# The first norm's weight as one row spread by two matmuls, and a reordered opening

## What is computed

```
h = rmsnorm(x, norm_mix_pre)           # x * rsqrt(mean(x^2) + 1e-6) * weight, row by row
P = h @ W_in                           # 1024 x 3584: seven groups of 512 columns
yA = block-sparse causal attention (8 heads, T5 relative bias) on three groups
yR = chunked retention (8 heads, group norm, swish gate) on four groups
x = x + rmsnorm(concat(yA, yR) @ W_out, norm_mix_post)
h = rmsnorm(x, norm_ffn_pre);  u = causal conv3(h @ W_up) + conv_b
x = x + rmsnorm((gelu(u_a) * u_b) @ W_down, norm_ffn_post)
```

## Time and profile before

| | us |
|---|---|
| median of 3 runs | 658.28 |
| lowest and highest | 658.04, 659.0 |
| the profiled execution, its device time | 657.82 |
| its span in the trace | 656.0 |
| PE busy | 637.3 (97% of the span) |
| DVE, ACT, POOL busy | 384.0, 299.4, 69.1 |

### The profile page before, as it was taken

How to read it: one execution, slowest core, us unless ns; L and a number is a source line. 1 busy time by engine, 2 the same in 40 slices (tenths; PEclk the granted TensorE clock), 3 DMA queues, 4 the chain that set the end, 5 groups by cost and what they waited for, 6 DMA issues and landing times.

```text
span 656.0 us, 9379 instructions
## 1 busy us (share of the span) xinstructions
PE 637.3 (97%) x3210; PEld 526.6 (80%) x3210; DVE 384.0 (59%) x565; ACT 299.4 (46%) x485; POOL 69.1 (11%) x88
## 2 busy tenths in 40 slices
PE   7999999999999899999999999999999999999996
PEld 7887877777787687899888888888888888878885
DVE  3448548646854975985755555555555654463455
ACT  5548327526733854664433333333333433362351
POOL 5402102111210302420000000000000000000002
PEclk9999999999999999999999999999999999999999
DMA  9634223331412145641433333333333023422323
GB/s 282 189 119 128 66 64 97 96 96 32 145 47 89 72 160 161 193 129 65 129 96 96 96 96 96 96 96 96 96 95 100 29 95 97 160 64 61 96 68 128
DMA packets 87110, 69.15 MB, mean 105 GB/s; under 512 B 2265, under 2 KB 76169, under 8 KB 87090
## 3 DMA queue, kind: packets, MB, share of 16 engines
q1 hardware_dynamic: 85618, 63.62, 32.2%
q0 software_dynamic: 1472, 5.26, 2.5%
HBM read 66.76 MB, written 2.12 MB: 105 GB/s over the span
## 4 chain that ended last, share of the span: by engine, by line
PE 83%; DVE 8%; ACT 3%; issue 3%; DMA 1%; POOL 1%; DVEq 0%; SPq 0%; POOLq 0%; ACTq 0%
PE bank L435 77%; PE bank L515 1%; DVE work L1165 1%; ACT work L827 1%; DMA raw<-in_w_in_dram 1%; DVE work L1174 1%; DVE ws L1048 1%; PE bank L578 1%; DVE yT L1094 1%; DVE work L1183 1%; PE bank L506 1%; DVE work L1184 1%; PE bank L505 1%; PE bank L446 1%; POOL ws L360 1%
## 5 line engine op out<-in xcount | busy, mean ns | idle before, releaser
L435 PE MATMUL bank<-hT,ws 128*128 128x512 f32 (+1 forms) x1872 | 412.4, 376 | 5.7 <-DVE work L1183 4.3
L435 PEld LDWEIGHTS bank<-hT,ws 128*128 128x128 f32 x1872 | 327.9, 188 | 67.1 <-issue 6.7
L435 PE MATMUL bank<-ws,yT 128*128 128x512 f32 x720 | 166.7, 390 | 0.3 <-PE bank L435 0.3
L435 PEld LDWEIGHTS bank<-ws,yT 128*128 128x128 f32 x720 | 134.3, 188 | 28.4 <-issue 1.1
L1048 DVE TENSOR_TENSOR ws<-raw,ws 128x1024 fp32r<-128x1024 f32 x85 | 103.5, 1218 | 6.9 <-ACT ws L768 6.4
L768 ACT ACTIVATE ws<-raw 128x1024 fp32r<-128x1024 f32 x88 | 92.5, 1052 | 15.5 <-PE bank L435 11.7
L1327 DVE TENSOR_TENSOR ws<-raw,ws 128x1024 fp32r<-128x1024 f32 x22 | 26.9, 1224 | 51.2 <-ACT ws L1008 51.2
L985 ACT ACTIVATE gains<-bank,conv 128x512 f32<-128x512 f32 x22 | 17.1, 779 | 75.0 <-PE bank L435 75.0
L1008 ACT ACTIVATE ws<-raw 128x1024 fp32r<-128x1024 f32 x22 | 23.3, 1057 | 56.2 <-PE bank L435 56.2
L985 ACT ACTIVATE rot<-bank,conv 128x512 f32<-128x512 f32 x22 | 17.1, 779 | 67.7 <-PE bank L435 67.7
L1304 DVE SCALAR_TENSOR_TENSOR gains<-bank,conv,gains 128x511 f32<-128x511 f32 x22 | 16.5, 750 | 52.8 <-ACT gains L985 52.8
(11 more groups left out here) (111 smaller groups left out, 477.4 us busy)
## 6 DMA issues: line engine op xcount, KB each, us to landing
raw<-in_w_up_dram SPq DMA_DIRECT2D x44, 512.0 KB, 3.8
raw<-in_w_in_dram SPq DMA_DIRECT2D x28, 512.0 KB, 4.4
raw<-in_w_down_dram SPq DMA_DIRECT2D x22, 512.0 KB, 3.9
raw<-in_w_out_dram SPq DMA_DIRECT2D x16, 512.0 KB, 3.6
xs<-in_x_dram SPq DMA_DIRECT2D x4, 512.0 KB, 6.4
work<-bias_vectors POOLq DMA_DIRECT2D x4, 512.0 KB, 3.9
work<-in_decay_dram POOLq DMA_DIRECT2D x4, 512.0 KB, 4.5
out_dram<-work SPq DMA_DIRECT2D x4, 256.0 KB, 2.0
```

The lines of the kernel that those rows point to most:

```text
L435: return nc.tensor.matmul(dst, st, mv, start=start, stop=stop)
```

## The change

`norm_mix_pre` is loaded as one row of 4 KB to partition 0, by ACT's own DMA queue, ahead of ACT's first activation. PE multiplies a column of 128 ones with each half of the row (two matmuls with a contraction of one, 512 columns each) into banks 6 and 7, and DVE copies the two halves to `gains`. The 512 KB load leaves SP's queue. `POOL_TO` goes from 3 to 1, so the low parts of units 1 and 2 are made by DVE instead of POOL. The squares of x tile 3 go from ACT to DVE (`tensor_tensor_reduce`). PE's warming matmuls go from 15, 2, 8 to 3, then behind the two spreading matmuls 7, 2, 4. Unit 1's `FRONT` goes ahead of the turn of tile 2.

```diff
-POOL_TO = 3
+POOL_TO = 1
...
+        ones = work[0:1, 9728:9728 + P]
+        x_squared = part(8704, 1024)
...
@@ SP
             load_x(1)
-            sp.dma_start(gains[:, 0, :], norm_mix_pre[0].partition_broadcast(P)).then_inc(gains_loaded, 16)
             load_turn(0, 0, 1)
...
@@ POOL
+            pool.memset(ones, 1.0).then_inc(ones_set, 1)
             pool.memset(neghalf[:], -0.5).then_inc(const_set, 1)
...
             x_rstd(2)
-            split_lo(1)
             x_rstd(3)
-            split_lo(2)
...
@@ PE
-            warm(15)
+            warm(3)
+            pe.wait_ge(gains_loaded, 16)
+            pe.wait_ge(ones_set, 1)
+            for half in range(2):
+                nc.tensor.matmul(bank[6 + half][:], ones, gains[0:1, 0, half * 512:half * 512 + 512],
+                                 start=True, stop=True).then_inc(gains_spread, 1)
+            warm(7)
             turn_rows(0)
             warm(2)
             turn_rows(1)
-            warm(8)
+            warm(4)
 
             pe.wait_ge(h_lo, 4)
             pe.wait_ge(w_lo_pool, 1)
             column_unit(0, bank[0], 0, 24, FRONT, False)
+            pe.wait_ge(w_lo, lo_count(1))
+            column_unit(1, bank[1], 0, 24, FRONT, False)
             turn_rows(2)
-            pe.wait_ge(w_lo_pool, 2)
-            column_unit(1, bank[1], 0, 24, FRONT, False)
             turn_rows(3)
...
@@ ACT
+            act.dma_start(gains[0:1, 0, :], norm_mix_pre[0:1, :]).then_inc(gains_loaded, 16)
             x_in(0)
...
             split_hi(1)
-            x_in(3)
             h_evacuate(2)
...
@@ DVE
-            dve.wait_ge(gains_loaded, 16)
+            for half in range(2):
+                dve.wait_ge(gains_spread, half + 1)
+                nc.vector.tensor_copy(gains[:, 0, half * 512:half * 512 + 512], bank[6 + half][:]).then_inc(gains_ready, 1)
+            dve.wait_ge(gains_ready, 2)
             normed_rows(0)
             normed_rows(1)
             h_low(0)
             h_low(1)
+            dve.wait_ge(x_loaded[3], 16)
+            dve.wait_ge(sq_done, 3)
+            nc.vector.tensor_tensor_reduce(out=x_squared, in0=xs[:, 3, :], in1=xs[:, 3, :], scale=1.0, scalar=0.0,
+                                           op0=ALU.mult, op1=ALU.add, accum_out=sumsq[:, 3:4]).then_inc(sq_done, 1)
             normed_rows(2)
+            split_lo(1)
             normed_rows(3)
             h_low(2)
             h_low(3)
+            split_lo(2)
```

More of the change, by code:

```diff
@@ L203, in build @@
         const_set = sem("const_set")
+        ones_set, gains_spread, gains_ready = sem("ones_set"), sem("gains_spread"), sem("gains_ready")
         low_cleared = sem("low_cleared")
```

## The result

| | before | changed |
|---|---|---|
| median of 12 runs, us | 657.95 | 660.36 |
| lowest to highest | 657.38 to 659.37 | 659.38 to 660.74 |
| ratio changed : before | | 1.0028 (95%: 1.002 to 1.0037) |
| profiled execution: device time, span | 657.82, 656.0 | 659.38, 657.6 |

The kernel became slower by about 0.3%, 1.8 us by the ratio; the two medians are 2.4 us apart. The forecast was no change (658.3), with 660.36 just inside the range of 657.1 to 660.5.

A forecast was written before the change was run, and what follows sets the result against it. PE was taken to bound the kernel, with only the opening before BACK (24.10 us) open to change. The terms summed to 24.1, so no change: 658.3 us on the median, chance 0.47, range 657.1 to 660.5.

The forecast's parts named there:

- What bounds: Whole kernel: PE is busy 97% of the span, and the end moves one for one with the BACK start, 24.10.
- The load leaves the queue: Opening DMAs: 512 KB less saves 1.5 to 2.3 us, so unit 0 lands at 7.6 to 8.4 instead of 9.92.
- The row arrives: Opening, ACT's queue: the 4 KB row, issued at about 0.75, lands at 2.75 to 4.05; 3.2 taken.
- land with x: Rival, opening: the row lands only at 4.05, DVE's rows start at 7.9, and the kernel takes 658.8 us; chance 0.10.
- The two matmuls: Opening, PE: the spreading matmuls start at 3.25, PE's pace rises at about 5.6, the second ends at 6.3, or 7.0 if slow.
- Tiles 0 and 1: Opening: ACT's fourth evacuation ends (E) 4.43 us after DVE's first rows start (G, 7.4), at 11.83.
- the pace stays low: Rival, opening: PE stays slow, warming matmuls last until 10.4; 662.3 us, or 660.3 if it rises at turn 0; chance 0.09.
- POOL beside DVE: Opening, tile 2: DVE's squares delay POOL's root, so DVE's rows start 1.9 us after ACT's squares end (S), not 1.3.
- POOL is not held up: Rival, opening: DVE's squares leave POOL alone, tile 2's rows start 0.6 us earlier, 657.7 us; chance 0.20.
- Low part of unit 1, and the turn behind it: Opening: unit 1's FRONT starts at S (ACT's tile 2 squares end) + 4.45, 17.3; BACK follows 6.75 us later, before 5.59.
- POOL in between: Rival, opening: POOL's low part of unit 0 runs between DVE's first two rows, up to 2.4 us late, 660.7 us; chance 0.08.
- The sum: BACK start: DVE's rows start (G) 7.4 + 4.43 + 1.04 + 4.45 + 6.75 = 24.1, as before.

The follow-up runs named there:

- e2: The changed kernel with four warming matmuls instead of seven behind the spreading ones; median 660.38 us, ratio to before 1.0030.
- e9: The changed kernel with POOL waiting for DVE's first two rows, tile 2's turn between the units and tile 3's squares on ACT; 658.35 us, ratio to before 1.0001.
- e1: The changed kernel without the seven warming matmuls behind the spreading ones; median 660.50 us, ratio to before 1.0035.
- e4: The changed kernel with the turn of tile 2 back between the FRONTs of units 0 and 1; median 658.94 us, ratio to before 1.0010.
- e5: The kernel before with only the row on ACT's queue, the spreading matmuls and their warming matmuls; median 658.97 us, ratio to before 1.0013.
- e7: The changed kernel with POOL waiting for both of DVE's first rows before unit 0's low part; median 659.74 us, ratio to before 1.0026.
- e6: The changed kernel with the weight loaded to all partitions by SP and 15, 2 and 8 warming matmuls, as before; 659.00 us, ratio to before 1.0008.
- e3: The changed kernel with spreading matmuls over all 128 rows, the weight's tile cleared first and the row loaded later; 662.29 us, ratio to before 1.0057.
- e10: The kernel before with its first 15 warming matmuls using one row of the array instead of 128; 659.58 us, ratio to before 1.0019.
- e8: The kernel before with only the low parts of units 1 and 2 moved to DVE; median 657.50 us, ratio to before 0.9990.
- e12: The kernel before with 20 first warming matmuls instead of 15; median 657.74 us, ratio to before 0.9991.
- e11: The kernel before with units 1 and 2's low parts on DVE and 20 first warming matmuls instead of 15; 657.16 us, ratio to before 0.9983.

## Why the prediction was right or wrong

Its map of the opening held; its forecast of no change did not. The measured slowdown lies among its cases with 0.14. The range held, but by 0.14 us and with some luck: the profiled execution, 659.38, lies above the 657.8 to 659.1 that the prediction gave for it, and what the range had room for was its rivals. Two of its own signs of being wrong came up: DVE's rows started after 8 us, and the seven warming matmuls lasted over 2 us (3.34).

- **What bounds.** Right. BACK moved by 1.55 us, the span by 1.6; the waits behind are the same to 0.1 us.
- **The load leaves the queue.** Right for the profiled run, and about right in the mean: unit 0 landed at 8.25, expected 7.6 to 8.4. In six others without the load it landed at 7.54 (e2), 7.75 (e9), 7.78 (e1), 8.41 (e4), 8.52 (e5) and 9.02 (e7), a wider spread than was allowed for.
- **The row arrives.** Taken as 3.2. PE began the spreading at 3.56 without an idle gap, so it was there by then. Harmless; what moved the spreading from 3.25 to 3.56 was the three warming matmuls. That it would land with x was not borne out in this run: tile 0's squares began at 4.29, when x had landed.
- **The two matmuls: the term that failed first.** "The second is a quarter done at 5.6 and ends at 6.3" took the moment of the rise from one run with other work on PE; in five runs of the old opening it lies between 5.3 and 7.5. The second ended at 7.3, both at low pace. The prediction had the other bound, 7.9 for DVE's rows, and even that was 0.2 too early, since PE began 0.3 later: they started at 8.10. The copies cost 0.69, as read from the earlier trace rows.
- **Tiles 0 and 1: the term that failed second.** E = G + 4.43 left out the seven warming matmuls. At 0.48 each they end at 10.6, 1.2 us behind tile 0's rows. E was 13.48, G + 5.38. The rival "the pace stays low" had exactly this, but to the end of the turns, and with 0.09.
- **POOL beside DVE.** Right, and well sized. The root's second instruction took 1.43 us and ended 0.4 us behind DVE's squares; tile 2's rows started at 16.34, 1.83 us behind S = 14.51, for the 1.9 taken. "POOL is not held up" is out.
- **Low part of unit 1, and the turn behind it.** Right: S + 4.31 (4.45 taken) and 6.83 us (6.75 taken). e6 and e4 show the second by itself.
- **POOL in between.** Had 0.08 in the prediction. The traces of e1 and e2 show it, and e3's has POOL ahead of both rows; in those of the changed kernel, e4 and e5 it did not happen. How often it happens in the changed kernel is not known. The argument against it was misread: in the earlier trace rows POOL asked when DVE's *first* instruction was 0.2 us old, and yet waited for both, so "POOL waits through adjacent instructions" seemed a rule. In e1 it asked 0.8 us into the first and got in before the second. What decides at a boundary is open: all that is shown is that POOL, asking at 8.67 and 8.91, got in, and asking at 9.39, after the second had started, did not.
- **The sum.** In the profiled run, 0.7 (G) + 0.95 (warming in the way) - 0.1 (the rest) = 1.55 us. Between that run and the median lies 1.0 us, and its cause stays open. Two candidates have the right size, by the end of the fourth evacuation, E, 13.48 in the profiled run: with POOL in between it is 14.51 in e1 (1.0 later), and with the turn of tile 0 at low pace 13.97 in e5, 14.16 in e4 and 14.82 in e9 (0.5 to 1.3 later). e7's median, 0.6 lower, is not clear of noise. No second execution of the changed kernel was profiled that could tell.

The two rules weighed before: the Trainium skill, "TensorE: Matmul & The Clock Gate", section on what is actually happening, says that activity lifts the clock from its default; e10 agrees only for matmuls with all rows: its one-row ones stayed at 421 ns, the all-row ones behind the turns came to 275. The Trainium skill, "SBUF — State Buffer", section on who interferes with whom, says that whichever starts first holds the other up for its whole instruction: e1 agrees, with 2.1 us added to DVE's two rows by a POOL instruction of 2.35 to 2.38 us, and so does e3, where POOL had begun first and DVE's row took 2.91 us instead of 1.28.

## What to carry to other kernels

Before a transfer is swapped for matmuls at the start of a program, read how fast PE runs there, and whether the new matmuls lift that pace or leave it low; they took twice the time per column of the nearest row, and so did the warming matmuls behind them. When a change lets data land earlier, ask which instructions of POOL and DVE that both read SBUF now meet, and in which order: here a POOL instruction added 2.1 us to two DVE rows in two runs with an early load, and in a third one wait kept it out. A step that is moved out of another engine's wait (the turn of tile 2) costs its full chain behind it, 1.2 us here. A gap of some 2 us on PE just ahead of the critical matmuls was worth filling: with five more warming ones the slow quarter of the runs was gone.

## What the runs showed of the hardware

- 15 float32 matmuls over one row and 128 columns kept the low pace for all of their 6.8 us (e10); with 128 rows and the same start at 1.85 the first fast records came between 5.3 and 7.5 us, in five traces.
- Until the pace first rises the clock column of the profile reads 1.00 all the same (rows 4, and 2 to 7 us of e8 above), while after the idle 2.45 us in e8 it reads 0.51, for a turn of the same 1.97 us as in e10, where the column still reads 1.00. Until then the length of the records tells the pace, not the column.
- An idle gap of 2.00 us on PE left the clock at 2.4 GHz in one run, one of 2.45 us saw it fall in another. Before's runs lie in two groups, 657.4 to 658.6 at a mean granted clock of 0.997 or more and 659.0 to 659.7 at 0.995 or 0.996; with five more matmuls the upper group is gone (e12, e11).
- A POOL instruction that reads SBUF and began first made a DVE instruction with SBUF inputs wait for it: 2.91 us for 1.28 (e3), and 4.58 us for two rows of 2.48, where POOL began between them (e1, e2). The other way round POOL took 3.41 us for 2.37 (the changed kernel).
- A 4 KB transfer took at most 2.8 us when issued at 0.73, and about 4.2 us when issued at 1.96 behind three 512 KB loads of another queue (e3).
